# Turning token tiles one by one, and scalar chains moved between quarters, in a hybrid block kernel

## The chip, the cores and the metric

The kernel runs on one core of a Trainium2 chip. The metric is the device time of one execution in microseconds (us); smaller is better. Engines are named as the profile names them: PE (matmul), DVE (VectorE), ACT (ScalarE), POOL (GpSimd), SP (SyncE, which only issues DMAs here). PEld is PE loading its stationary operand.

## What is computed

One layer of a hybrid backbone on 512 latent tokens and 256 context tokens of width 2048, all float32. The part that the change touches is the start:

```
mod_x = silu(c) @ w_ada + b_ada          # (1, 6144): shift, scale, gate
mod_c = silu(c_ctx) @ w_ada + b_ada
h_x = rmsnorm(x, g_pre) * (1 + sc_x) + sh_x       # 512 tokens
h_c = rmsnorm(ctx, g_pre) * (1 + sc_c) + sh_c     # 256 tokens
parts_x = split(h_x @ w_in)                       # u, xa, ba, ca, za, zb, f, zc, gates
u_c = h_c @ w_in[:, u]
a = exp((lam_re + i lam_im) * exp(log_dt))        # 2 x 64 x 64 poles; q = (a - 1) / lam
```

Behind it come a gated convolution, a bidirectional diagonal state-space scan with a GLU, a 2-D Fourier mix, three projections, gates, one output projection, an RMS norm and the residual. They are not touched.

## The kernel before

Products are made three times over, high times high, low times high and high times low, from operands split into a rounded part (`hi`, made by ACT) and the rest (`lo`, made by DVE).

**The opening.** The modulation needs 4 quarters of 512 channels. Quarter q takes eight units of `w_ada`, each 256 rows x 1024 columns (1 MB, two DMAs of 512 KB) in a ring of four buffers, `ring`; SP issues unit n once unit n-4 is used. `ada(n)` (L578, its matmuls are L586) multiplies one unit. After the eighth, ACT copies the sums to `rows` (`rows_cp`), PE turns them to columns (`cols`, L593), and DVE adds the bias and makes shift and scale (`columns(q)`, L1433 to L1438). `ada(8*(q+1))` waits until `columns(q)` has read the bank.

**Tokens.** x arrives in four tiles of 128 tokens (`xn`, 1 MB each), ctx in two (`cn`). ACT squares each tile with a row sum (L1011), DVE makes mean plus epsilon (L1361), ACT the root (L1013), DVE inverts it with one correction step (L1353 to L1357), and ACT scales the tile (L1016). Before the change this is done for all four tiles of x at a time. `early_turn(k)` then turns channel block k of all four tiles (L602) into a PSUM bank of `ac`, and ACT copies it out to `xT` (L1019), for the first 12 of 16 blocks; the last four are turned in quarter 3 by `turn`.

**A quarter of the first product.** For block n of quarter q DVE does `modulate` (L1451; L1455 for ctx), ACT `high`, DVE `low` (L1464); n = 0 to 3 is x, 4 and 5 is ctx. PE does `x_piece(q, r)` (L633, L634, L637) and `c_piece(q, r)` (L650, L651, L653), both with weight units 2q and 2q+1, which ACT rounds (`hi_first`) and DVE subtracts (`lo_first`, L1468). These are units of 512 KB in `wslot`, the first eight issued by SP among the units of `w_ada`. Between the pieces PE takes the ada units of the next quarter.

**Scalar chains on DVE.** The poles need exp, sine and cosine, made of small linked instructions on 128 x 64 elements. Before: both exponentials (L1345, L1347) and the first half of the sines (L1365 to L1374) run ahead of the one `token_scale` for x, the second half (L1377 to L1382) and the cosines (L1386 to L1390) behind it; `zoh` (L1394 to L1408) stands in quarter 0 before its two ctx blocks, `chunk_powers` (L1411 to L1424) at the end of quarter 0. Their results are first read by PE in `p0_z` (L662), behind quarter 3's x pieces.

The order on every engine is the order of the program text; engines meet at semaphores. After the opening come the phases of 'stream', each product one weight unit after another.

Of the kernel before, what the change touches and what calls it, by code (L numbers as in the profile page):

```python
# [24 lines left out]
ALU = mybir.AluOpType  # L25
# [74 lines left out]
def program(nc, x, c, ctx, c_ctx, w_ada, b_ada, g_pre, g_post, w_in, conv_w, lam_re, lam_im, log_dt,  # L100
# [37 lines left out]
    EARLY = 12  # L138
# [52 lines left out]

    hch = at("hch", [128, KD, TC], abr_at, F32R)
    drow = at("drow", [G, L, H], abr_at)
    junk = at("junk", [128, D], abr_at + KD // 2 * TC * 4)
    last4 = (KD - 4) * T * 4
    ring = [at(f"ring{n}", [128, 2, 2, 512], off)
            for n, off in enumerate((hx_at + last4, hxl_at + last4, tab_at, tab_at + 8192))]
# [23 lines left out]
    r = Region(abr_at + 4 * TC * 4)  # L221
    crow = r("crow", [2 * KD, 128])
    vrow = r("vrow", [V_END, 128])
    lam = r("lam", [128, 2, P])
    ldt = r("ldt", [128, 1])
    zt = [r(f"zt{i}", [128, P]) for i in range(8)]
    ei = r("ei", [128, P], I32)
    assert r.p <= abr_at + KD // 2 * TC * 4

    bah = at("bah", [128, KW, T], abr_at, F32R)  # L230
    fT = at("fT", [128, KW * T], abr_at)
# [129 lines left out]
    def _(sp):  # L361
# [19 lines left out]
            sp.dma_start(xn[:, t, :], x[0, t * 128:(t + 1) * 128, :]).then_inc(x_in[t], 16)  # L381
        for n in range(32):
            ada_unit(n)
            if n % 8 >= 6:
                first_unit(n // 8 * 2 + n % 2)
            if n in (8, 9):
                sp.dma_start(cn[:, n - 8, :], ctx[0, (n - 8) * 128:(n - 7) * 128, :]).then_inc(c_in, 16)
# [183 lines left out]
    def _(pe):  # L571
# [6 lines left out]
        def ada(n):  # L578
            q, r = n // 8, n % 8
            if r == 0 and q:  # L580
                pe.wait_ge(col_rd, q)
            pe.wait_ge(ada_in[n % 4], 32 * (n // 4 + 1))
            for kk in range(2):
                for h in range(2):
                    p = 64 * kk + 32 * h
                    last = mm(ss[p:p + 2, 2, :], cs[:, 2 * r + kk, :], ring[n % 4][:, kk, h, :],  # L586
                              start=(r == 0), stop=(r == 7))
            last.then_inc(ada_used, 1)
# [5 lines left out]
                          sel[:, :, :].rearrange("p h s -> p (h s)"), start=True, stop=True)  # L594
            last.then_inc(col_ps, 1)

        def early_turn(k):
            pe.wait_ge(y_done, TT)
            if k >= 4:
                pe.wait_ge(xp_done, k - 3)  # L600
            for t in range(TT):
                last = tr(ac[:, k % 4, t * 128:(t + 1) * 128], xn[:, t, k * 128:(k + 1) * 128], ident[:, :])  # L602
            last.then_inc(xp_ps, 1)

        def turn(q, n):
            if q == 3 or n == 5:
# [73 lines left out]
            last.then_inc(p0_ps, 1)  # L680

        for n in range(8):
            ada(n)
            if n == 3:
                pe.wait_ge(vec_in, 64)
                tr(ss[:, 1, 0:V_END], vrow[:, :], ident[0:V_END, 0:V_END])
                tr(ss[:, 1, 128:128 + G], drow[:, :, :].rearrange("n l h -> n (l h)"), ident[0:G, 0:G]).then_inc(vec_ps, 1)
            if 3 <= n < 7:
                for k in range(3 * (n - 3), 3 * (n - 2)):
                    early_turn(k)  # L690
        cols(0)
        ada(8)
        ada(9)
        pe.wait_ge(xp_done, EARLY)
        for r in range(4):
            x_piece(0, r, range(4))
            ada(10 + r)
        turn(0, 4)
        ada(14)
        turn(0, 5)  # L700
        for q in range(3):
            if q:
                x_piece(q, 0, range(4))
# [265 lines left out]
    def _(act):  # L969
# [26 lines left out]
        def hi_first(u):  # L996
            if u >= 2:
                act.wait_ge(w_used, u - 1)
            act.wait_ge(w_in_s[u % NSLOT], 16 * (u // NSLOT + 1))
            cp(whi[:, u % 2, :], wslot[:, u % NSLOT, :]).then_inc(w_hi, 1)  # L1000
# [5 lines left out]
            act.wait_ge(w_in_s[s], arrived)  # L1006
            cp(whi[:, (U0[k] + j) % 2, :], wslot[:, s, :]).then_inc(w_hi, 1)

        for t in range(TT):
            act.wait_ge(x_in[t], 16)  # L1010
            st.link(a(junk[:, :], toks[t], ACT.Square, accum_out=small[:, 32 + t:33 + t]))  # L1011
        act.wait_ge(var_done, 1)
        a(small[:, 46:50], small[:, 40:44], ACT.Sqrt).then_inc(rt_done, 1)  # L1013
        act.wait_ge(rs_done, 1)
        for t in range(TT):
            cp(toks[t], toks[t], small[:, 52 + t:53 + t]).then_inc(y_done, 1)  # L1016
        for k in range(EARLY):
            act.wait_ge(xp_ps, k + 1)
            cp(xT[:, k, :], ac[:, k % 4, :]).then_inc(xp_done, 1)  # L1019
            if k == 8:  # L1020
                hi_first(0)
        hi_first(1)
        rows_cp(0)
        for n in range(4):
            high(0, n)
        act.wait_ge(c_in, 32)
        for t in range(TT, TT + CT):
            st.link(a(junk[:, :], toks[t], ACT.Square, accum_out=small[:, 32 + t:33 + t]))
        act.wait_ge(var_done, 2)
        a(small[:, 50:52], small[:, 44:46], ACT.Sqrt).then_inc(rt_done, 1)  # L1030
        act.wait_ge(rs_done, 2)
        for t in range(TT, TT + CT):
            cp(toks[t], toks[t], small[:, 52 + t:53 + t]).then_inc(y_done, 1)
        high(0, 4)
# [258 lines left out]
        act.wait_ge(w_in_s[unit(8, 3, 7)[1]], unit(8, 3, 7)[2])  # L1293
        cp(whx[:, :], wslot[:, unit(8, 3, 7)[1], :]).then_inc(w_hi, 1)
        a(small[:, 63:64], ident[:, 0:1], ACT.Sqrt)
        act.wait_ge(var_done, 3)
        for t in range(TT):
            act.wait_ge(ac_done, 9 + t + 1)
            act.wait_ge(sq_done, 12 + t)
# [6 lines left out]
    def _(dve):  # L1306
# [35 lines left out]
        dve.wait_ge(ssm_in, 48)  # L1342
        a0, a1, a2, a3, a4, a5, a6, a7 = [z[:, :] for z in zt]
        lre, lim = lam[:, 0, :], lam[:, 1, :]
        exp(a7[:, 0:1], ldt[:, :], a1[:, 0:1], a2[:, 0:1], a3[:, 0:1], a4[:, 0:1], ei[:, 0:1])  # L1345
        link(ts_(a0, lre, a7[:, 0:1], None, ALU.mult))
        exp(a6, a0, a1, a2, a3, a4, ei[:, :])  # L1347

        def rsqrt(at, n, rt):

            dve.wait_ge(rt_done, rt)
# [7 lines left out]
        def token_scale(at, n, turn):  # L1359
# [2 lines left out]
                .then_inc(var_done, 1)  # L1362
            dve.wait_ge(var_done, turn)
            rsqrt(at, n, turn).then_inc(rs_done, 1)
        link(ts_(a0, lim, a7[:, 0:1], None, ALU.mult))  # L1365
        nearest(a1, a0, 1.0 / math.pi)
        link(stt(a2, a1, -3.140625, a0, ALU.mult, ALU.add))
        link(stt(a2, a1, -9.67502593994140625e-4, a2, ALU.mult, ALU.add))
        link(stt(a2, a1, -1.509957990978376432e-7, a2, ALU.mult, ALU.add))
        nearest(a3, a1, 0.5)  # L1370
        link(stt(a3, a3, -2.0, a1, ALU.mult, ALU.add))
        link(tt(a3, a3, a3, ALU.mult))
        link(ts_(a3, a3, -2.0, 1.0, ALU.mult, ALU.add))
        link(tt(a1, a2, a2, ALU.mult))  # L1374
        fact = [1.0 / math.factorial(n) for n in range(16)]
        token_scale(0, TT, 1)
        link(ts_(a4, a1, fact[13], -fact[11], ALU.mult, ALU.add))  # L1377
        for cc in (fact[9], -fact[7], fact[5], -fact[3], 1.0):
            link(tt(a4, a4, a1, ALU.mult))
            link(ts_(a4, a4, cc, None, ALU.add))  # L1380
        link(tt(a4, a4, a2, ALU.mult))
        link(tt(a4, a4, a3, ALU.mult))  # L1382
        dve.wait_ge(vec_ps, 1)
        cpy(dtab[:, :], ss[:, 1, 128:128 + G])
        link(cpy(vecs[:, :], ss[:, 1, 0:V_END]))
        link(ts_(a5, a1, -fact[14], fact[12], ALU.mult, ALU.add))  # L1386
        for cc in (-fact[10], fact[8], -fact[6], fact[4], -fact[2], 1.0):
            link(tt(a5, a5, a1, ALU.mult))
            link(ts_(a5, a5, cc, None, ALU.add))
        link(tt(a5, a5, a3, ALU.mult))  # L1390
        z = lambda n: ZN[:, n, 0, :]

        def zoh():
# [75 lines left out]
                .then_inc(w_lo, 1)  # L1469

        for q in range(4):
            if q == 0:
                lo_first(0)
            columns(q)
            modulate(q, 0)
            low(q, 0)
            modulate(q, 1)
            low(q, 1)
            if q:
                lo_first(2 * q)  # L1480
            modulate(q, 2)
            low(q, 2)
            modulate(q, 3)
            low(q, 3)
            lo_first(2 * q + 1)
            if q == 0:
                token_scale(TT, CT, 2)
                zoh()
            for n in range(4, 6):
                modulate(q, n)  # L1490
                low(q, n)
            if q == 0:
# [408 lines left out]
        u, s, _ = unit(8, 3, 7)  # L1901
        dve.wait_ge(w_hi, u + 1)
        tt(wlo[:, s, :], wslot[:, s, :], whx[:, :].bitcast(F32), ALU.subtract).then_inc(w_lo, 1)
        dve.wait_ge(var_done, 3)
        dve.wait_ge(xr_in, 64)
        for t in range(TT):
            dve.wait_ge(sq_done, 12 + t + 1)
            tt(Og[:, t, 1536:2048], ss[:, t, :], GG[:, 1536:2048], ALU.mult).then_inc(o_free, 1)
            s40, s46, s52, s58 = (small[:, c0 + t:c0 + t + 1] for c0 in (40, 46, 52, 58))
            link(ts_(s40, ssq[:, 4 * t + 3:4 * t + 4], 1.0 / D, s58, ALU.mult, ALU.add))  # L1910
            dve.wait_ge(rt_done, 3 + t)
            link(v.reciprocal(s52, s46))
# [51 lines left out]
```

## Time and profile before

| | us |
|---|---|
| median of three executions | 2057.66 (2055.9 to 2057.74) |
| profiled execution, device time | 2056.32 |
| its span, first to last instruction | 2054.5 |
| PE busy | 2008.0 (98%) |
| DVE busy | 1085.9 (53%) |
| ACT busy | 594.9 (29%) |
| moved by DMA | 270.72 MB, mean 132 GB/s |

A row of the profile's timeline gives the start and duration in us, the engine, line and operation, written tile <- read tiles, and in brackets how long the engine had been idle and what ended that. A number x8 is a count of instructions merged into the row. Durations of matmuls overlap a little.

### The profile page before, as it was taken

The numbers are of one execution on the slowest core, as the hardware profiler recorded it, in microseconds if no ns is written. First come the engines' busy times: TensorE is split into PE (matmuls) and PEld (weight loads), VectorE is DVE, ScalarE is ACT, GpSimd is POOL, SyncE is SP. The second block draws the span as 40 slices with busy tenths as digits, with TensorE's granted clock in tenths as the row PEclk, the third lists the DMA queues.
The fourth block names the chain that finished last, engine by engine and source line by source line (L and its number), as shares of the span: only waits on it lengthen the run. The fifth ranks groups of instructions, "written<-read, shape, count | busy, mean of one in ns | idle before, by whom it ended". The sixth has DMA issues, their size and how long they took to land.

```text
span 2054.5 us, 26821 instructions
## 1 busy us (share of the span) xinstructions
PE 2008.0 (98%) x10086; PEld 1639.5 (80%) x10086; DVE 1085.9 (53%) x1640; ACT 594.9 (29%) x845; POOL 27.0 (1%) x16
## 2 busy tenths in 40 slices
PE   4999999999999999999999999999999999999998
PEld 1568888888888888888888888888788888888886
DVE  4545799999998645554334344432433333333325
ACT  5325243334333322222222222222322222222222
POOL 0003100000000000000000000000000000000000
PEclk9999999999999999999999999999999999999999
DMA  9963544434344544443334444443233333334423
GB/s 360 365 199 115 167 108 109 104 103 112 98 110 111 179 133 127 128 136 107 102 92 145 127 128 139 129 133 112 62 93 100 95 95 99 93 101 153 173 99 128
DMA packets 384079, 270.72 MB, mean 132 GB/s; under 512 B 24820, under 2 KB 349916, under 8 KB 382164
## 3 DMA queue, kind: packets, MB, share of 16 engines
q1 hardware_dynamic: 373728, 265.61, 41.9%
q10 hardware_dynamic: 10292, 4.33, 1.5%
q8 instruction: 36, 0.59, 0.1%
q14 instruction: 23, 0.19, 0.0%
HBM read 251.81 MB, written 18.09 MB: 131 GB/s over the span
## 4 chain that ended last, share of the span: by engine, by line
PE 93%; DVE 3%; ACT 2%; DMA 1%; issue 1%; SPq 0%; ACTq 0%; DVEq 0%
PE ac L753 25%; PE ac L757 25%; PE ac L754 24%; PE ac L937 1%; PE ac L938 1%; PE ac L936 1%; PE ss L815 1%; PE ss L586 1%; PE ss L938 1%; PE ss L937 1%; PE ss L936 1%; PE ac L633 1%; PE ac L634 1%; PE ac L637 1%; DMA wslot<-w_in 1%
## 5 line engine op out<-in xcount | busy, mean ns | idle before, releaser
L1556 DVE TENSOR_TENSOR wlo<-wslot,whi 128x1024 fp32r<-128x1024 f32 x309 | 378.4, 1224 | 643.4 <-ACT whi L972 639.2
L972 ACT ACTIVATE whi<-wslot 128x1024 fp32r<-128x1024 f32 x327 | 346.9, 1061 | 1244.7 <-PE ac L757 1043.7
L753 PE MATMUL ac<-hxh,whi 128*128 128x512 f32 x1664 | 651.9, 392 | 0.0
L754 PE MATMUL ac<-hxl,whi 128*128 128x512 f32 x1664 | 647.8, 389 | 0.0
L757 PE MATMUL ac<-hxh,wlo 128*128 128x512 f32 x1664 | 411.1, 389 | 0.9 <-DVE wlo L1556 0.9
L753 PEld LDWEIGHTS ac<-hxh,whi 128*128 128x128 f32 x1664 | 312.4, 188 | 67.5 <-issue 2.9
L757 PEld LDWEIGHTS ac<-hxh,wlo 128*128 128x128 f32 x1664 | 312.2, 188 | 66.1 <-DVE wlo L1556 1.3
L754 PEld LDWEIGHTS ac<-hxl,whi 128*128 128x128 f32 x1664 | 312.4, 188 | 63.8
L753 PE MATMUL ac<-bah,whi 128*128 128x512 f32 x384 | 149.4, 389 | 0.0
L754 PE MATMUL ac<-bal,whi 128*128 128x512 f32 x384 | 149.4, 389 | 0.0
L757 PE MATMUL ac<-bah,wlo 128*128 128x512 f32 x384 | 94.8, 389 | 0.0
L753 PEld LDWEIGHTS ac<-bah,whi 128*128 128x128 f32 x384 | 72.1, 188 | 15.0
L754 PEld LDWEIGHTS ac<-bal,whi 128*128 128x128 f32 x384 | 72.1, 188 | 15.0
L757 PEld LDWEIGHTS ac<-bah,wlo 128*128 128x128 f32 x384 | 72.1, 188 | 15.0
L753 PE MATMUL ac<-b2nd,whi 128*128 128x512 f32 x192 | 74.8, 390 | 0.0
L754 PE MATMUL ac<-b2nd,whi 128*128 128x512 f32 x192 | 74.7, 389 | 0.0
L1775 DVE TENSOR_TENSOR gtm<-ac,gsig 128x512 f32<-128x512 f32 x32 | 22.1, 691 | 85.7 <-PE ac L757 85.7
L586 PE MATMUL ss<-ring,cs 128*2 128x512 f32 x256 | 38.1, 676 | 24.1 <-DMA ring<-w_ada 20.8
L1731 DVE SCALAR_TENSOR_TENSOR gacc<-gwt,cs,gacc 128x256 f32<-128x256 f32 x120 | 57.8, 481 | 3.4
L936 PE MATMUL ac<-whi,mhi 128*128 128x512 f32 x128 | 50.2, 392 | 0.0
L938 PE MATMUL ac<-whi,mlo 128*128 128x512 f32 x128 | 49.8, 389 | 0.0
L937 PE MATMUL ac<-wlo,mhi 128*128 128x512 f32 x128 | 49.8, 389 | 0.0
(359 smaller groups left out, 2075.1 us busy)
## 6 DMA issues: line engine op xcount, KB each, us to landing
wslot<-w_in SPq DMA_DIRECT2D x224, 512.0 KB, 3.8
ring<-w_ada SPq DMA_DIRECT2D x64, 512.0 KB, 8.3
gwt<-w_ada SPq DMA_DIRECT2D x128, 128.0 KB, 2.8
wslot<-w_out SPq DMA_DIRECT2D x32, 512.0 KB, 3.6
wslot<-proj_a SPq DMA_DIRECT2D x16, 512.0 KB, 4.1
wslot<-proj_b SPq DMA_DIRECT2D x16, 512.0 KB, 4.1
wslot<-proj_c SPq DMA_DIRECT2D x16, 512.0 KB, 3.9
xn<-x SPq DMA_DIRECT2D x4, 1024.0 KB, 9.7
```

Source lines behind the costliest of these rows:

```text
L586: last = mm(ss[p:p + 2, 2, :], cs[:, 2 * r + kk, :], ring[n % 4][:, kk, h, :], start=(r == 0), stop=(r == 7))
L633: mm(ac[:, m, :], w, hxh[:, k, :], start=(k == 0), stop=False)
L753: mm(ac[:, bank, :], w, xh, start=(v == 0 and q == 0), stop=False)
L754: mm(ac[:, bank, :], w, xl, start=False, stop=False)
L757: last = mm(ac[:, bank, :], wlo[:, s, q * 128:(q + 1) * 128], rhs(v * UNIT + q)[0], start=False, stop=(v == nu - 1 and q == UNIT - 1))
L936: mm(acc[:, t, :], mh, wh, start=(kk == 0), stop=False)
L937: mm(acc[:, t, :], mh, wl, start=False, stop=False)
L938: last = mm(acc[:, t, :], ml, wh, start=False, stop=(kk == KD - 1))
L972: cp = lambda o, i, scale=1.0: nc.scalar.activation(o, i, ACT.Copy, scale=scale)
L1556: tt(wlo[:, s, :], wslot[:, s, :], whi[:, (U0[k] + j) % 2, :].bitcast(F32), ALU.subtract)\
L1731: stt(gacc[:, :], gwt[:, r % 4, :], cs[:, r, 0:1], gacc[:, :], ALU.mult, ALU.add)\
L1775: tt(o if br == 0 else gtm2[:, :], ac[:, (2 * j + 1) % 4, :], gsig[:, :], ALU.mult)\
```

## The change

Four things change. ACT, DVE and PE treat each tile of x by itself: square, root, scale, then twelve transposes of that tile into three banks, `early_turn(t)`, and three copies out. Six banks rotate, four of `ac` and two of `ss`. On PE these stand before ada(0), before ada(1), after ada(2) and after ada(4), and ada(9) moves behind the first x piece (each of the next ones one place later). On SP weight units 0 and 1 both go behind unit 7 of `w_ada`. On ACT and DVE the splits of weight units 0 and 1 move: `hi_first(0)` behind `rows_cp(0)` and ahead of the first `high`, `lo_first(0)` behind the first `modulate`. On DVE the token scales come first, then the exponentials; sines stand at the end of quarter 0, cosines and `zoh` at the end of quarter 1, `chunk_powers` at the end of quarter 2. Two scratch areas move so that they stay free that long.

```diff
-    junk = at("junk", [128, D], abr_at + KD // 2 * TC * 4)
+    junk = at("junk", [128, D], VT_at + KD // 2 * TC * 4)
...
             ada_unit(n)
-            if n % 8 >= 6:
+            if n == 7:
+                first_unit(0)
+                first_unit(1)
+            if n > 8 and n % 8 >= 6:
                 first_unit(n // 8 * 2 + n % 2)
...
-        def early_turn(k):
-            pe.wait_ge(y_done, TT)
-            if k >= 4:
-                pe.wait_ge(xp_done, k - 3)
-            for t in range(TT):
-                last = tr(ac[:, k % 4, t * 128:(t + 1) * 128], xn[:, t, k * 128:(k + 1) * 128], ident[:, :])
-            last.then_inc(xp_ps, 1)
+        PARTS = EARLY // 4
+
+        def early_bank(n):
+            return (ac[:, n % 6, :] if n % 6 < 4 else ss[:, 3 * (n % 6 - 4), :])
+
+        def early_turn(t):
+            pe.wait_ge(y_done, t + 1)
+            for g in range(PARTS):
+                n = t * PARTS + g
+                if n >= 6:
+                    pe.wait_ge(xp_done, n - 5)
+                for k in range(4):
+                    c0 = (4 * g + k) * 128
+                    last = tr(early_bank(n)[:, k * 128:(k + 1) * 128], xn[:, t, c0:c0 + 128], ident[:, :])
+                last.then_inc(xp_ps, 1)
...
         for n in range(8):
+            if n in (0, 1):
+                early_turn(n)
             ada(n)
+            if n in (2, 4):
+                early_turn(n // 2 + 1)
...
-            if 3 <= n < 7:
-                for k in range(3 * (n - 3), 3 * (n - 2)):
-                    early_turn(k)
         cols(0)
         ada(8)
-        ada(9)
-        pe.wait_ge(xp_done, EARLY)
+        pe.wait_ge(xp_done, TT * PARTS)
         for r in range(4):
             x_piece(0, r, range(4))
-            ada(10 + r)
+            ada(9 + r)
         turn(0, 4)
+        ada(13)
+        turn(0, 5)
         ada(14)
-        turn(0, 5)
...
+        token_square(0)
+        token_root(0)
+        token_square(1)
+        token_norm(0)
+        token_root(1)
+        token_square(2)
+        token_norm(1)
+        token_root(2)
+        token_square(3)
+        token_norm(2)
+        token_root(3)
+        early_out(0)
+        token_norm(3)
+        for t in range(1, TT):
+            early_out(t)
+        rows_cp(0)
+        hi_first(0)
+        high(0, 0)
+        high(0, 1)
         hi_first(1)
-        rows_cp(0)
-        for n in range(4):
-            high(0, n)
+        high(0, 2)
+        high(0, 3)
...
+        for t in range(TT):
+            token_scale(t, 1, t + 1)
+        exp(a7[:, 0:1], ldt[:, :], a1[:, 0:1], a2[:, 0:1], a3[:, 0:1], a4[:, 0:1], ei[:, 0:1])
+        link(ts_(a0, lre, a7[:, 0:1], None, ALU.mult))
+        exp(a6, a0, a1, a2, a3, a4, ei[:, :])
...
         for q in range(4):
+            columns(q)
+            modulate(q, 0)
             if q == 0:
                 lo_first(0)
-            columns(q)
-            modulate(q, 0)
             low(q, 0)
...
             if q == 0:
-                token_scale(TT, CT, 2)
-                zoh()
+                token_scale(TT, CT, TT + 1)
             for n in range(4, 6):
                 modulate(q, n)
                 low(q, n)
             if q == 0:
+                sines()
+            if q == 1:
+                cosines()
+                zoh()
+            if q == 2:
                 chunk_powers()
```

## Rows read from the trace of the kernel before

**Rows 1.** The page: busy time of each engine, its share of the span, and instructions.

```profile
PE 2008.0 (98%) x10086; PEld 1639.5 (80%) x10086; DVE 1085.9 (53%) x1640; ACT 594.9 (29%) x845; POOL 27.0 (1%) x16
```

**Rows 2.** Stretches: length, busy (count), clock share, DMA share, GB/s.

```profile
48.00:50.00 2.00, 0.48 (x4) 0.11 (x8) 1.31 (x3) 0.63 (x1) 0.00 (x0) 0.50 0.96 395
...
7.00:76.50 69.50, 49.41 (x276) 24.50 (x276) 35.52 (x144) 38.27 (x43) 0.00 (x0) 0.95 1.04 389
...
80.00:100.00 20.00, 20.00 (x125) 12.08 (x122) 8.93 (x15) 5.05 (x7) 0.00 (x0) 1.00 0.94 337
```

**Rows 3.** Timeline of PE at unit 24 and at the last quarter's wait.

```profile
106.74 0.61 PE L586 MATMUL ss<-ring,cs 128*2 128x512 f32 x4
...
144.22 0.50 PE L637 MATMUL ac<-hxh,wlo 128*128 128x512 f32 x1 [2.12 <-DVE wlo L1468]
```

**Rows 4.** Timeline of DVE at columns(2) and columns(3).

```profile
105.32 0.24 DVE L1433 TENSOR_TENSOR vmod<-ss,vecs 128x8 f32<-128x8 f32 x2 [3.75 <-PE ss L593]
...
132.79 0.24 DVE L1433 TENSOR_TENSOR vmod<-ss,vecs 128x8 f32<-128x8 f32 x2 [3.75 <-PE ss L593]
```

**Rows 5.** Timeline of ACT, the squares, the table load, roots and scales.

```profile
7.72 1.91 ACT L1011 ACTIVATE junk<-xn 128x2048 f32<-128x2048 f32 x1 [1.39 <-DMA xn<-x]
...
21.02 1.28 ACT L1013 ACT_TABLE_LOAD   x1 [2.97 <-DVE small L1361]
...
23.63 7.68 ACT L972 ACTIVATE xn<-xn,small 128x2048 f32<-128x2048 f32 x4 [1.11 <-DVE small L1357]
...
53.29 1.90 ACT L1028 ACTIVATE junk<-cn 128x2048 f32<-128x2048 f32 x1
...
57.61 0.20 ACT L1030 ACTIVATE small<-small 128x2 f32<-128x2 f32 x1 [0.30 <-DVE small L1361]
```

**Rows 6.** Timeline of PE, transposes, and ada(9), ada(10), ada(11) with x pieces between.

```profile
31.36 2.82 PE L602 MATMUL ac<-ident,xn 128*128 128x128 f32 x12 [0.94 <-ACT xn L972]
...
49.52 1.89 PE L586 MATMUL ss<-ring,cs 128*2 128x512 f32 x8 [1.96 <-DMA ring<-w_ada]
...
55.58 1.04 PE L586 MATMUL ss<-ring,cs 128*2 128x512 f32 x8
...
59.49 1.04 PE L586 MATMUL ss<-ring,cs 128*2 128x512 f32 x8
```

**Rows 7.** Second DMA of units 7, 15, 19: last figures are issue start and landing time.

```profile
L367 SPq DMA_DIRECT2D ring<-w_ada x1: 472/472/472, 30.3 to 30.3; - x1
DMA to landing us min/median/max: 9.8/9.8/9.8
...
L367 SPq DMA_DIRECT2D ring<-w_ada x1: 472/472/472, 61.0 to 61.0; - x1
DMA to landing us min/median/max: 8.6/8.6/8.6
...
L367 SPq DMA_DIRECT2D ring<-w_ada x1: 472/472/472, 72.2 to 72.2; - x1
DMA to landing us min/median/max: 9.5/9.5/9.5
```

**Rows 8.** Timeline of PE at units 15 and 16.

```profile
70.70 1.04 PE L586 MATMUL ss<-ring,cs 128*2 128x512 f32 x8
...
79.29 0.61 PE L586 MATMUL ss<-ring,cs 128*2 128x512 f32 x4 [2.95 <-DVE vmod L1433]
```

**Rows 9.** Stretches of the scalar chains: sines (two), cosines, zoh, chunk_powers.

```profile
17.78:20.77 2.99, 1.85 (x8) 0.14 (x8) 2.58 (x12) 0.27 (x2) 0.00 (x0) 1.00 1.05 386
23.51:26.69 3.18, 2.35 (x16) 0.11 (x8) 2.74 (x14) 3.06 (x2) 0.00 (x0) 1.00 1.05 386
30.93:34.34 3.41, 2.98 (x16) 2.53 (x20) 2.94 (x14) 1.69 (x4) 0.00 (x0) 1.00 1.05 386
58.79:62.97 4.18, 4.18 (x23) 2.51 (x22) 3.67 (x16) 3.90 (x2) 0.00 (x0) 1.00 1.05 386
73.67:79.01 5.34, 2.67 (x23) 2.46 (x22) 4.69 (x23) 0.00 (x0) 0.00 (x0) 1.00 1.05 387
```

More of the change, by code:

```diff
@@ L223, in program @@
     vrow = r("vrow", [V_END, 128])
+    assert r.p <= abr_at + KD // 2 * TC * 4
+    r = Region(abr_at + 12 * TC * 4)
     lam = r("lam", [128, 2, P])
@@ L227, in program @@
     ei = r("ei", [128, P], I32)
-    assert r.p <= abr_at + KD // 2 * TC * 4
+    assert r.p <= abr_at + KD * TC * 4
     bah = at("bah", [128, KW, T], abr_at, F32R)
@@ L1007, in hi, with token_square, token_root, token_norm @@
             cp(whi[:, (U0[k] + j) % 2, :], wslot[:, s, :]).then_inc(w_hi, 1)
-        for t in range(TT):
+        def token_square(t):
             act.wait_ge(x_in[t], 16)
             st.link(a(junk[:, :], toks[t], ACT.Square, accum_out=small[:, 32 + t:33 + t]))
[L1012 to L1015, printed above, removed]
-            cp(toks[t], toks[t], small[:, 52 + t:53 + t]).then_inc(y_done, 1)
[L1017 to L1021, printed above, removed]
+        def token_root(t):
+            act.wait_ge(var_done, t + 1)
+            a(small[:, 46 + t:47 + t], small[:, 40 + t:41 + t], ACT.Sqrt).then_inc(rt_done, 1)
+        def token_norm(t):
+            act.wait_ge(rs_done, t + 1)
+            cp(toks[t], toks[t], small[:, 52 + t:53 + t]).then_inc(y_done, 1)
+        def early_out(t):
+            for g in range(EARLY // 4):
+                n = t * (EARLY // 4) + g
+                act.wait_ge(xp_ps, n + 1)
+                bank = ac[:, n % 6, :] if n % 6 < 4 else ss[:, 3 * (n % 6 - 4), :]
+                cp(xT[:, 4 * g:4 * g + 4, t * 128:(t + 1) * 128], bank.rearrange("p (k c) -> p k c", k=4))\
+                    .then_inc(xp_done, 1)
+        token_square(0)
[17 more added lines that the diff above has]
+        high(0, 1)
         hi_first(1)
-        rows_cp(0)
-        for n in range(4):
-            high(0, n)
+        high(0, 2)
+        high(0, 3)
         act.wait_ge(c_in, 32)
@@ L1028, in _ @@
             st.link(a(junk[:, :], toks[t], ACT.Square, accum_out=small[:, 32 + t:33 + t]))
-        act.wait_ge(var_done, 2)
+        act.wait_ge(var_done, TT + 1)
         a(small[:, 50:52], small[:, 44:46], ACT.Sqrt).then_inc(rt_done, 1)
-        act.wait_ge(rs_done, 2)
+        act.wait_ge(rs_done, TT + 1)
         for t in range(TT, TT + CT):
@@ L1295, in _ @@
         a(small[:, 63:64], ident[:, 0:1], ACT.Sqrt)
-        act.wait_ge(var_done, 3)
+        act.wait_ge(var_done, TT + 2)
         for t in range(TT):
@@ L1344, in _ @@
         lre, lim = lam[:, 0, :], lam[:, 1, :]
-        exp(a7[:, 0:1], ldt[:, :], a1[:, 0:1], a2[:, 0:1], a3[:, 0:1], a4[:, 0:1], ei[:, 0:1])
-        link(ts_(a0, lre, a7[:, 0:1], None, ALU.mult))
-        exp(a6, a0, a1, a2, a3, a4, ei[:, :])
         def rsqrt(at, n, rt):
@@ L1364, in token_scale @@
             rsqrt(at, n, turn).then_inc(rs_done, 1)
[L1365 to L1382, printed above, removed]
+        for t in range(TT):
[3 more added lines that the diff above has]
+        exp(a6, a0, a1, a2, a3, a4, ei[:, :])
         dve.wait_ge(vec_ps, 1)
@@ L1385, in _, with sines, cosines @@
         link(cpy(vecs[:, :], ss[:, 1, 0:V_END]))
[L1386 to L1390, printed above, removed]
+        def sines():
+            link(ts_(a0, lim, a7[:, 0:1], None, ALU.mult))
+            nearest(a1, a0, 1.0 / math.pi)
+            link(stt(a2, a1, -3.140625, a0, ALU.mult, ALU.add))
+            link(stt(a2, a1, -9.67502593994140625e-4, a2, ALU.mult, ALU.add))
+            link(stt(a2, a1, -1.509957990978376432e-7, a2, ALU.mult, ALU.add))
+            nearest(a3, a1, 0.5)
+            link(stt(a3, a3, -2.0, a1, ALU.mult, ALU.add))
+            link(tt(a3, a3, a3, ALU.mult))
+            link(ts_(a3, a3, -2.0, 1.0, ALU.mult, ALU.add))
+            link(tt(a1, a2, a2, ALU.mult))
+            fact = [1.0 / math.factorial(n) for n in range(16)]
+            link(ts_(a4, a1, fact[13], -fact[11], ALU.mult, ALU.add))
+            for cc in (fact[9], -fact[7], fact[5], -fact[3], 1.0):
+                link(tt(a4, a4, a1, ALU.mult))
+                link(ts_(a4, a4, cc, None, ALU.add))
+            link(tt(a4, a4, a2, ALU.mult))
+            link(tt(a4, a4, a3, ALU.mult))
+        def cosines():
+            fact = [1.0 / math.factorial(n) for n in range(16)]
+            link(ts_(a5, a1, -fact[14], fact[12], ALU.mult, ALU.add))
+            for cc in (-fact[10], fact[8], -fact[6], fact[4], -fact[2], 1.0):
+                link(tt(a5, a5, a1, ALU.mult))
+                link(ts_(a5, a5, cc, None, ALU.add))
+            link(tt(a5, a5, a3, ALU.mult))
         z = lambda n: ZN[:, n, 0, :]
@@ L1903, in _ @@
         tt(wlo[:, s, :], wslot[:, s, :], whx[:, :].bitcast(F32), ALU.subtract).then_inc(w_lo, 1)
-        dve.wait_ge(var_done, 3)
+        dve.wait_ge(var_done, TT + 2)
         dve.wait_ge(xr_in, 64)
@@ L1910, in _ @@
             link(ts_(s40, ssq[:, 4 * t + 3:4 * t + 4], 1.0 / D, s58, ALU.mult, ALU.add))
-            dve.wait_ge(rt_done, 3 + t)
+            dve.wait_ge(rt_done, TT + 2 + t)
             link(v.reciprocal(s52, s46))
```

## The prediction

> **What bounds the kernel now.** I read the page's totals first: PE is busy for 98% of the span [rows 1], so the whole kernel can gain only where PE stands still, which is 46.5 us in all. Next I read stretches of the opening, where the change lies. From 7 to 76.5 us the DMA engines are full (share 1.04, 389 GB/s) while PE works 49.4 of 69.5 us; from 80 us on PE works without a gap and DMA falls below full [rows 2]. Later, at 144, PE waits again, for DVE. The opening therefore has three limits one after the other: the first DMA queue until some 77 us, then PE, then at the start of the last quarter the pair DVE and ACT.
>
> The third limit is read from PE's row at 144.22: it stood 2.12 us for the low part of weight unit 7 (DVE L1468) [rows 3]. That wait ends a chain which starts at the column step of the last quarter at 132.79 and goes through modulate, rounding on ACT and subtraction on DVE four times [rows 4]. Whatever moves 132.79 moves the rest of the kernel.
>
> **The change part by part, front end.** Before, ACT squares four token tiles as they land (first at 7.72), loads a table at 21.02, scales all four in 7.68 us from 23.63, and only then PE turns them at 31.36 [rows 5, 6]. After the change the rhythm of ACT, with durations from those rows, is: square 0 to 9.7; DVE; table load 1.28 and root to 11.5; square 1 to 13.5; scale 0 (7.68 / 4 = 1.92) to 15.4; then root, square, scale in turn; scale 2 ends at 23.7, copies out of tile 0 (three, 1.6) at 25.4, scale 3 at 27.4, copies of tile 1 at 29.0. PE turns tile 0 from 15.4 to 18.2 (2.82 for twelve [rows 6]), before unit 0 of w_ada is there at all, tile 1 behind ada(0), tile 2 behind ada(2), tile 3 behind ada(4), done by about 35.5. Nothing is saved in number: 48 transposes and 12 copies of 512 columns in both. What is gained is that ada(1) to ada(6) are eaten as they land, and the rest of the turning lies in waits for the DMA queue. DVE pays five small instructions and two waits per tile in place of per four, some 1.3 us each, in ACT's shadow; the two exponentials that now stand behind them (about 10 us) end near 35, and the next DVE work, columns(0), comes after 41, so they cost nothing.
>
> Weight units 0 and 1 now go behind unit 7 instead of one ahead of it. Unit 7 landed at 30.3 + 9.8 = 40.1 [rows 7]; it is 512 KB, 1.35 us, earlier: 38.7. Weight units land at 40.1 and 41.4, later units as before. So ada(7) ends at 39.7, rows and cols(0) at 41.5, columns(0) at 42.0. ACT rounds weight unit 0 at 40.4 to 41.5, ahead of the first high, so nothing is queued badly behind that wait. low(0,0) is done at 44.4 (lo_first(0) now sits ahead of it, 1.2 us), and ada(8), which lands at 44.1, is eaten until 46.0, at the low clock after PE's gap. The first x piece starts at 46.0 instead of 51.4, behind ada(9) at 49.52 + 1.89 [rows 6]: some 5.3 us sooner, partly because ada(9), for which PE waited 1.96 us at 49.52, now stands behind it.
>
> **Why these 5.3 us don't last.** The queue of w_ada was full and in order until 77 us, and carries the same bytes in the same order. Unit 15 landed at 61.0 + 8.6 = 69.6 and unit 19 at 72.2 + 9.5 = 81.7 [rows 7]. Walking PE on with its own durations (x piece and ada 3.91, from 55.58 to 59.49 [rows 6], of it ada 0.97 with the overlap): x pieces 0 to 3 with ada(9) to ada(12) end at 63.6 (the first piece at the low clock, 4.3, and 0.4 us of waiting for unit 10), the two ctx turns and ada(13), ada(14) at 67.0. Then PE waits 2.6 us for unit 15 and ends it at 70.6, where before it ended at 71.7 [rows 6, 8]. The 5.3 us have become 1.1. What is still to be had is the gap at 79.29, where PE stood 2.95 us for DVE, which had chunk_powers (5.34 us) ahead of columns(1) [rows 8, 9]. Sines take its place there: 2.99 + 3.18 = 6.17 us [rows 9], 0.8 more. But they start sooner: the ctx turns come 4.7 us sooner, so DVE is free at 69.0, through with sines at 75.1, and ada(16) can start at 75.4, just as PE comes to it. That is 3.9 us sooner than 79.29. Unit 19, at 81.7, then sets the end: ada(19) ends at 82.65 instead of at 86.3. So 3.65 us are gained on entering the second quarter, and no more than this, since the queue sets it.
>
> **The back end, where it is given back.** cosines (3.41) and zoh (4.18), 7.59 us together [rows 9], move from the first quarter, where they lay beside waits, to between low(1,5) and columns(2). DVE's idle time ahead of columns(2) is 3.75 us [rows 4], so columns(2) comes 3.84 us after its natural place, at 105.32 + 3.84 - 3.65 = 105.5. PE needs it for ada(24): that ran at 106.74 [rows 3], 1.14 us after the 105.60 at which the columns were read, and now comes at 105.8. PE's lead shrinks from 3.65 to 0.95. Then chunk_powers, 5.34 us, stands ahead of columns(3), again in an idle stretch of 3.75 us [rows 4]: 1.59 us too long. This delay falls right on the third limit. Columns(3) comes at 132.79 + 1.59 - 0.95 = 133.4. Sum: 3.84 - 1.14 + 1.59 - 3.65 = **+0.64 us**. I take nothing for what follows: the chain of that quarter has the same instructions, and ZN is ready long before p0_z.
>
> Unknown prices. The early copies out write 128-column pieces at a stride instead of one run; from no extra to double (0.5 us each), they stay in ACT's slack ahead of 39.7. PE's clock in the new order isn't in the trace: nothing to 2.6 us, below. The lead could be 0.5 us more if the queue's rate varies; a gain beyond the queue is excluded, because bytes and order are the same.
>
> Two rules of the Trainium skill speak against parts of this. ScalarE: Activation LUTs, section "Table sets: the hidden batching unit", says to batch activations by set and not by function, since a change of set costs a load. The rows show Square at 53.29 and 55.31 and Sqrt at 57.61 with no load between, after the one at 21.02 [rows 5], so alternating costs none here; with a load at each of six changes, 6 x 1.28 = 7.7 us, tile 3 would be turned by 43 and the first x piece would start some 3 us later, which the wait for unit 15 takes up. DMA: Bandwidth & Descriptors, section "Specifications", gives about 358 GB/s from HBM for a core; an estimate from that page would land unit 19 six us later. The trace disagrees with 389 GB/s, and the measurement decides.
>
> **Rivals.**
> Low clock, slower: in the trace PE fell to half clock (0.50 at 48 to 50 us) after broken work around 44 to 49 and was back near 55 [rows 2, 6]. The new order has new gaps, at 41.5 to 44.1 and at 67.0 to 69.6. One spell after the second gap, as long as the old one, costs about 2.5 us: 2060.0. If instead the clock stays low through the x pieces, each piece with its ada takes 7.1 instead of 3.9 us, by the ratio of the two adas at either level (1.89 to 1.04 [rows 6]); four cost 12.8, less 2.6 of waiting: 10.2 later than the forecast, 2067.7. It decides from the point at which two of the four pieces run low. Against it: the same pieces brought the clock back within one piece before, and 2.95 us of idling at 76 to 79 didn't lower it. 9% for over +4.1, 10% for the one spell.
> The gaps are as wide as the moved chains: then 3.65 us stay, 2053.3, just inside 0.2%. Against it are the two idle times of 3.75 us [rows 4]. 6%.
> The queue doesn't bind: the 5.3 us, and the 2.12 us at 144, are kept: 2051.6 to 2049.5. Against it is a full DMA share until 77. 5%.
>
> **How the numbers follow.** 0.2% is 4.1 us, about what a measurement of this kernel can tell from no change. The profiled execution took 2056.32 us (span 2054.5, 1.8 around it), 1.3 below the median 2057.66; the mean of the four executions shown is 2056.9. With +0.64 on it: **2057.5 us**, essentially no change, 70%. Same is 70 + 10 + 6 less a little for scatter at the edges: 82%. Faster 7%, slower 11%. The range goes from the rival that keeps its gain, with a little scatter, to the one clock spell with 1 us of scatter: 2053.5 to 2061.5.
>
> **What would show it.** Right: first x piece near 46; PE waits 2 to 3 us for ring ahead of ada(15); no idle of PE for vmod near 75; ada(24) waits about 2.7 us for DVE's column step (vmod); DVE has no idle time ahead of columns(2) and columns(3); the wait for the low part of weight unit 7 ends at 144.9 or so. Wrong: PE still idle for DVE in the first quarter, half clock over more than one piece between 46 and 70, or the last quarter's columns well before 132.

## The result

The changed kernel takes 2061.85 us (median of 22 executions, 2059.03 to 2064.23), the kernel before 2058.51 us (22, 2055.90 to 2062.93). The ratio is 1.0014, with a 95% interval from 1.0008 to 1.0020: slower by some 3 us. The forecast was 2057.5 us and no change, with a range that ended at 2061.5. The time lies above the range. Two executions of the kernel before in the later comparisons, at 4160 and 6281 us, are left out of every figure below.

The traces are of single executions. That of the kernel before took 2056.32 us, 2.2 us under its median, and that of the kernel after 2059.82 us, 2.0 us under its own, so the two can be set beside each other, and both are on the fast side.

Read beside the first rows is the page of the kernel after: its span, then busy time of each engine. PE is busy 2.5 us more [rows 1] with the same 10086 instructions, and stands still 1.0 us more.

```profile
span 2058.0 us, 26840 instructions
...
PE 2010.5 (98%) x10086; PEld 1643.3 (80%) x10086; DVE 1088.7 (53%) x1658; ACT 594.9 (29%) x848; POOL 27.0 (1%) x16
```

The same instructions, busy for longer in sum, point to some of them having run slower. The timeline of ACT in the kernel after shows the new opening; it answers rows 5.

```profile
7.21 1.91 ACT L1025 ACTIVATE junk<-xn 128x2048 f32<-128x2048 f32 x1 [0.73 <-DMA xn<-x]
...
9.55 1.28 ACT L1029 ACT_TABLE_LOAD   x1 [0.34 <-DVE small L1396]
...
12.97 2.00 ACT L986 ACTIVATE xn<-xn,small 128x2048 f32<-128x2048 f32 x1
...
24.45 2.01 ACT L986 ACTIVATE xn<-xn,small 128x2048 f32<-128x2048 f32 x1
```

One table load, then square, root and scale in turn, without another load. The timeline of PE in the kernel after, which answers rows 6, 8 and 3:

```profile
44.07 1.89 PE L591 MATMUL ss<-ring,cs 128*2 128x512 f32 x8 [1.02 <-DMA ring<-w_ada]
46.02 0.77 PE L646 MATMUL ac<-hxh,whi 128*128 128x512 f32 x1
...
69.39 1.04 PE L591 MATMUL ss<-ring,cs 128*2 128x512 f32 x8 [2.72 <-DMA ring<-w_ada]
...
105.62 1.51 PE L591 MATMUL ss<-ring,cs 128*2 128x512 f32 x8 [2.57 <-DVE vmod L1477]
...
117.14 1.04 PE L591 MATMUL ss<-ring,cs 128*2 128x512 f32 x8
...
146.06 0.50 PE L650 MATMUL ac<-hxh,wlo 128*128 128x512 f32 x1 [2.13 <-DVE wlo L1512]
...
157.84 0.93 PE L675 MATMUL ss<-ident,ZN 128*128 128x128 f32 x7
```

Read down the idle times in brackets. The first x piece starts at 46.0, 5.3 us sooner than before, where its first matmul was at 51.33. PE waits 2.72 us for unit 15. ada(16), at 75.07 and without a bracket, no longer waits. ada(24) waits 2.57 us for DVE's columns. p0_z, the first work behind the opening, starts at 157.84; in the kernel before it started at 154.38. These 3.46 us are the whole difference of the spans, 2058.0 - 2054.5: from p0_z to the end both kernels take the same time, 1900.1 and 1900.2 us.

The timeline of DVE in the kernel after, at columns(2) and columns(3), answers rows 4: there is no idle time ahead of either, so no bracket.

```profile
105.33 0.24 DVE L1477 TENSOR_TENSOR vmod<-ss,vecs 128x8 f32<-128x8 f32 x2
...
134.39 0.42 DVE L1468 COPY ZN<-ZN 128x448 f32<-128x448 f32 x1
134.74 0.22 DVE L1477 TENSOR_TENSOR vmod<-ss,vecs 128x8 f32<-128x8 f32 x2
```

columns(2) is where it was before, 105.33 for 105.32. columns(3) is 1.95 us later.

What is new is in the stretches. The columns are those of rows 2; the third figure from the end is the granted clock of PE. First the kernel after, then the kernel before over the same work (from ada(24) to ada(28), and from the last quarter's wait to p0_z).

```profile
106.00:109.40 3.40, 3.40 (x19) 2.34 (x12) 2.01 (x4) 2.21 (x3) 0.00 (x0) 0.51 0.28 74
...
147.00:150.40 3.40, 3.40 (x12) 2.78 (x11) 1.47 (x3) 0.63 (x1) 0.00 (x0) 0.50 0.00 0
...
105.62:117.14 11.52, 11.52 (x68) 6.74 (x68) 7.11 (x11) 4.42 (x6) 0.00 (x0) 0.85 0.71 238
146.06:157.84 11.78, 11.78 (x49) 9.62 (x50) 3.38 (x6) 2.84 (x5) 0.00 (x0) 0.86 0.01 1
```

```profile
106.74:116.72 9.98, 9.98 (x69) 5.68 (x68) 6.41 (x9) 4.13 (x6) 0.00 (x0) 1.00 0.82 270
...
144.22:154.38 10.16, 10.16 (x48) 8.35 (x49) 3.37 (x6) 2.84 (x5) 0.00 (x0) 1.00 0.01 2
```

Soon behind each of the two waits, of 2.57 and 2.13 us, PE ran at half clock (0.50, the 1.2 GHz level) for a while. It began 0.4 us after the first wait had ended and 1.0 us after the second. The same work took 11.52 us for 9.98 and 11.78 for 10.16: 1.54 and 1.62 us more. The kernel before had a wait of 2.12 us at the second place too [rows 3], and in its profiled execution no half clock behind it.

The 3.46 us of p0_z are then: ada(24) 1.12 sooner, 1.54 of low clock, 1.42 lost between ada(28) and the end of the last quarter's wait (1.84 late there, 0.42 at ada(28)), and 1.62 of low clock: -1.12 + 1.54 + 1.42 + 1.62 = 3.46. The 1.42 is chunk_powers' excess, forecast at 1.59.

### The profile page after: what moved, and what is told of

Its sections match the earlier page's. It is cut to its first block, busy times and chain, and to the rows that moved or that the text cites. A ratio compares the mean times of both kernels' runs of the same rounds, so it can differ in the third digit from the quotient of the medians.

```text
span 2058.0 us, 26840 instructions
## 1 busy us (share of the span) xinstructions
PE 2010.5 (98%) x10086; PEld 1643.3 (80%) x10086; DVE 1088.7 (53%) x1658; ACT 594.9 (29%) x848; POOL 27.0 (1%) x16
## 4 chain that ended last, share of the span: by engine, by line
PE 91%; DMA 4%; DVE 3%; ACT 1%; issue 1%; SPq 1%; DVEq 0%; ACTq 0%
PE ac L767 25%; PE ac L771 25%; PE ac L768 24%; DMA ring<-w_ada 3%; PE ac L951 1%; PE ac L952 1%; PE ac L950 1%; PE ss L829 1%; PE ss L952 1%; PE ss L951 1%; PE ss L950 1%; PE ss L591 1%; DMA wslot<-w_in 1%; PE ss L822 1%; PE ac L646 1%
## 5 line engine op out<-in xcount | busy, mean ns | idle before, releaser
L951 PE MATMUL ss<-wlo,mhi 128*128 128x512 f32 x128 | 49.8, 389 | 0.0
```

Source lines behind the costliest of these rows:

```text
L951: mm(acc[:, t, :], mh, wl, start=False, stop=False)
```

## The experiments

The theory after the result (A) has three parts: the front end gives what was forecast; the chains cost what was forecast, because DVE's idle stretches at the ends of the quarters are shorter than the chains are; and the rest is half clock behind PE's waits. Rivals: B, turning tile by tile upsets what follows and the chains are harmless; C, the half clock has another cause than these waits, or costs nothing.

**The front end alone.** The changed kernel, with the chains called where they had been:

```diff
+        sines()
         dve.wait_ge(vec_ps, 1)
         cpy(dtab[:, :], ss[:, 1, 128:128 + G])
         link(cpy(vecs[:, :], ss[:, 1, 0:V_END]))
+        cosines()
...
                 token_scale(TT, CT, TT + 1)
+                zoh()
...
-            if q == 0:
-                sines()
-            if q == 1:
-                cosines()
-                zoh()
-            if q == 2:
-                chunk_powers()
+            if q == 0:
+                chunk_powers()
```

> The changed kernel with the scalar chains called where the kernel before had them: sines and cosines ahead of columns(0), zoh ahead of the ctx blocks of quarter 0, chunk_powers at its end. Nothing is left out. Theory A (the chains in the narrow gaps cost 2.70 and 1.59 us, and the two spells of half clock behind PE's waits at 103 and 144 us cost 1.4 and 1.6): the lead of the front end, 3.65 us on entering quarter 1, is kept to the end, PE doesn't wait ahead of ada(24), no half clock at 106 to 109; 3 to 4 us below before, ratio 0.998 to 0.9985. Theory B (turning tile by tile itself upsets what follows, the chains are harmless): ratio stays at 1.001.

Measured: 2056.0 us (11 executions), ratio 0.9985 (0.9976 to 0.9995), as expected by theory A. The front end is a gain, and PE doesn't wait ahead of ada(24). But the expectation said that the lead is kept to the end, and in the profiled execution it isn't, for its stretches show half clock again, at other places:

```profile
71.60:78.40 6.80, 6.80 (x36) 6.28 (x38) 5.40 (x22) 0.92 (x2) 0.00 (x0) 0.50 1.05 386
...
143.40:146.60 3.20, 3.20 (x10) 2.53 (x10) 0.59 (x2) 0.00 (x0) 0.00 (x0) 0.50 0.00 0
```

The first is behind the wait for unit 15. With it ada(16) starts at 78.00, where in the kernel after it starts at 75.07. The second is behind the last quarter's wait, and p0_z comes at 154.89, 0.5 us later than in the kernel before. B falls, for it has the ratio stay at 1.001 here.

**The chains alone.** The kernel before with the same four blocks at the ends of quarters 0, 1 and 2 and the two scratch areas moved with them. Nothing of the front end.

> The kernel before with the scalar chains alone moved, as in the change. Nothing is left out. Theory A: 0.8 us later in quarter 0 (6.17 for 5.34), 2.7 at ada(24), 1.6 at columns(3), together 5.1, and 1 to 3 us of half clock: 5 to 8 us above before, ratio 1.0025 to 1.004. Theory B: within 1 us of before.

Measured: 2065.6 us (6 executions, 2065.20 to 2067.43), ratio 1.0031 (1.0019 to 1.0043), some 6 us more, within the 5 to 8 that theory A expected. Waits of PE in its timeline:

```profile
79.45 1.13 PE L588 MATMUL ss<-ring,cs 128*2 128x512 f32 x8 [3.79 <-DVE vmod L1439]
...
110.98 1.89 PE L588 MATMUL ss<-ring,cs 128*2 128x512 f32 x8 [2.56 <-DVE vmod L1439]
```

3.79 for 2.95 in quarter 0 is the 0.8 us of sines over chunk_powers; 2.56 is the 2.7 at ada(24), and its 1.89 us for eight matmuls is the low clock. Its profiled execution has three such spells, behind these two waits and behind the last quarter's, of 2.12 us:

```profile
80.20:83.60 3.40, 3.40 (x20) 2.74 (x20) 2.03 (x4) 2.21 (x3) 0.00 (x0) 0.51 0.59 145
110.98:114.40 3.42, 3.42 (x15) 1.71 (x16) 2.00 (x5) 2.21 (x3) 0.00 (x0) 0.50 0.17 16
151.80:155.20 3.40, 3.40 (x12) 2.77 (x11) 0.99 (x2) 0.26 (x1) 0.00 (x0) 0.52 0.00 0
```

The two parts add up: -0.0015 and +0.0031 make +0.0016, and the whole change gives +0.0014. Each of these carries an uncertainty of about 0.001, so an interplay of more than some 3 us between the parts is excluded, and a smaller one isn't.

**PE's waits filled.** PE gets matmul work that nobody reads, in a PSUM bank that is free then, just ahead of the wait. It takes nothing away and costs nothing as long as it ends before the wait does; in this run 0.38 us of the wait ahead of ada(24) are left behind it.

```diff
+            if n == 24:
+                pe.wait_ge(ht_done, 12)
+                for _ in range(20):
+                    tr(ss[:, 3, 0:128], ident[:, :], ident[:, :])
             if r == 0 and q:
                 pe.wait_ge(col_rd, q)
...
+            if q == 3 and r == 2 and ms == (0,):
+                pe.wait_ge(col_rd, 4)
+                for _ in range(16):
+                    tr(ss[:, 2, 0:128], ident[:, :], ident[:, :])
             pe.wait_ge(w_lo, u + 1)
```

> The changed kernel; PE fills two of its waits with transposes that nobody reads: 20 ahead of its wait for columns(2) before ada(24) (2.4 of 2.57 us), 16 ahead of its wait for the low part of weight unit 7 in the last quarter (1.9 of 2.13 us). Theory A: the granted clock stays at full level at 106 to 109 us and 146 to 150 us; ada(28) starts some 1.4 us sooner than at 117.14, and the whole is 2.5 to 3 us below the changed kernel, within 1 us of before. Rival C (half clock comes from something else than these waits, or their cost is hidden by DVE): same time as the changed kernel, ratio 1.0014, and the clock falls as before or its fall costs nothing.

Measured: 2060.56 us (11), ratio 1.0007 (0.9998 to 1.0016). Both spells are gone from the profiled execution and p0_z is at 155.96, but a new one sits behind the wait for unit 15, which was not filled, so that ada(16) starts at 76.79 for 75.07:

```profile
71.30:74.70 3.40, 3.40 (x17) 3.36 (x16) 2.92 (x15) 0.12 (x1) 0.00 (x0) 0.50 1.06 388
```

The expectation of 2.5 to 3 us was met by half, and the profiled execution shows a place for the rest. So the third wait was filled as well, by 20 transposes into a bank of `ss` ahead of the wait for unit 15:

> The changed kernel; PE fills three waits: 20 transposes at unit 15 (2.4 of 2.6 us), 20 ahead of ada(24), 16 in the last quarter. Nobody reads them. Theory A: with no half clock between 60 us and the last product, only the walk of the prediction is left, +0.64 us against the kernel before without half clock: p0_z near 155.0, and 0.5 to 1 us above before_filled. Rival (the front end or the chains cost more than their durations): 2 us or more above before_filled.

Measured: 2058.37 us (11), ratio 0.9999 (0.9990 to 1.0008). Its stretches show full clock throughout the opening:

```profile
62.00:110.00 48.00, 46.85 (x327) 29.46 (x326) 28.92 (x87) 10.35 (x15) 0.00 (x0) 1.00 0.96 351
...
100.00:140.00 40.00, 37.42 (x260) 26.54 (x258) 25.21 (x70) 8.55 (x13) 0.00 (x0) 1.00 0.76 237
140.00:160.00 20.00, 19.62 (x121) 17.15 (x122) 10.54 (x29) 6.66 (x10) 0.20 (x1) 1.00 0.12 32
```

p0_z is at 154.79. Against 154.38 in the profiled execution of the kernel before, which was free of half clock after 60 us, that is +0.4 us, where the walk of the forecast gave +0.64. This is no sharp test, for single executions of one kernel are shifted against each other by as much: ada(24) starts at 105.62 in one trace of the changed kernel and at 106.39 in the other. Three fillers took the ratio of the changed kernel from 1.0014 (1.0009 in the second measurement, below) to 0.9999, 2 to 3 us, without taking any work away, and the spells behind these waits are gone from the trace. C falls.

**The kernel before filled.** 23 transposes ahead of ada(16)'s wait, 16 in the last quarter.

> The kernel before; PE fills two of its waits with transposes that nobody reads: 23 ahead of its wait for columns(1) at ada(16) (2.7 of 2.95 us), 16 ahead of the wait for the low part of weight unit 7 (1.9 of 2.12 us). If half clock behind these waits, now here and now there, is what spreads the executions of the kernel before over 2055 to 2063 us, this one lies at 2055.5 to 2058 with less spread, ratio 0.999. If not, the same median and spread as before.

Measured: 2056.53 us (11 executions, 2055.88 to 2057.98), ratio 0.9990 (0.9981 to 0.9999), beside 2058.05 (2055.71 to 2063.02) of the unfilled one on the same chip. So the kernel before has such spells too in many executions, and few of them in its fastest. The mean granted clock that is recorded with every execution says the same: among the 31 of the kernel before in this comparison it was 0.997 or 0.998 where they took 2055.7 to 2057.9 us, and 0.993 where they took 2062.6 to 2063.0. Likewise the 22 of the changed kernel go from 0.996 at 2059.8 us to 0.991 at 2064.2. The mean says how much low clock there was, not where. The four executions from which the forecast started, with a mean of 2056.9, were on the lucky side.

after_filled3 lies 1.8 us above before_filled, over the 0.5 to 1 that was expected, and close to the rival's 2 or more. In the profiled executions p0_z is no later for it, 154.79 against 155.16, so the difference isn't seen in the opening. Its executions fall in two groups, four at 2056.3 to 2056.8, level with before_filled, and seven at 2058.3 to 2059.2. The profiled execution is of the lower group. The next two kernels show a place for the 2 us between the groups.

**chunk_powers alone moved.** It is called in quarter 2 ahead of the ctx blocks, in place of behind them; otherwise as after_filled3.

> after_filled3 with chunk_powers alone moved from the end of quarter 2 to ahead of its ctx blocks, where DVE idled 5.72 us. Theory A: columns(3) is ready when PE's cols(3) is, 1.6 us sooner, and all that follows with it: 1.6 us below after_filled3. If the last quarter is set by PE and not by DVE's chain: 0.

Measured: 2056.65 us (11), ratio 0.9991 (0.9982 to 1.0000), 1.7 us below after_filled3, where 1.6 were expected; columns(3) at 132.10 for 133.28, and p0_z at 153.66 for 154.79. This execution had started ada(24) 0.4 us later; counted from there, columns(3) is 1.6 us sooner and p0_z 1.5. Its executions fall in two groups as well, of five and six, and the profiled one, of the slower group, has half clock at a place outside the opening, behind a wait of 1.94 us ahead of the Fourier products:

```profile
1455.20:1458.60 3.40, 3.40 (x19) 3.40 (x18) 1.05 (x6) 0.72 (x3) 0.00 (x0) 0.52 0.11 32
```

after_filled3's profiled execution has the same wait and full clock behind it.

**The chains in the wide stretches.** DVE idles longest ahead of the ctx blocks, while PE works on x pieces 0 and 1.

```diff
             if q == 0:
                 token_scale(TT, CT, TT + 1)
+                sines()
+            if q == 1:
+                zoh()
+            if q == 2:
+                chunk_powers()
             for n in range(4, 6):
                 modulate(q, n)
                 low(q, n)
             if q == 0:
-                sines()
-            if q == 1:
                 cosines()
-                zoh()
-            if q == 2:
-                chunk_powers()
```

> The changed kernel with the chains in DVE's wide idle stretches, that ahead of the ctx blocks: sines (6.17 us) in quarter 0 ahead of block 4 (6.66 idle), cosines (3.41) at the end of quarter 0 (4.6 idle), zoh (4.18) in quarter 1 ahead of block 4 (4.96 idle), chunk_powers (5.34) in quarter 2 ahead of block 4 (5.72 idle). Theory A: all of it is hidden, the lead of 3.65 us is kept, columns(3) starts near 129.1: 3.5 to 4.5 us below before, ratio 0.998. Theory B: ratio 1.000 or above. If half clock spells stay without the waits: some 1.5 us less gain.

Measured: 2056.53 us (11 executions, 2052.49 to 2058.84), ratio 0.9987 (0.9977 to 0.9997). Expected were 3.5 to 4.5 us, measured 2.0 to 2.7. The timeline of DVE shows that the chains are hidden, with idle time left behind each: sines, cosines (ahead of columns(1)), `zoh` and chunk_powers, in this order:

```profile
64.35 1.00 DVE L1499 TENSOR_SCALAR htmp<-ss,vmod 128x256 f32<-128x256 f32 x2 [0.64 <-PE ss L633]
...
75.46 0.24 DVE L1477 TENSOR_TENSOR vmod<-ss,vecs 128x8 f32<-128x8 f32 x2 [3.14 <-PE ss L598]
...
92.78 0.99 DVE L1499 TENSOR_SCALAR htmp<-ss,vmod 128x256 f32<-128x256 f32 x2 [1.72 <-PE ss L633]
...
120.16 1.00 DVE L1499 TENSOR_SCALAR htmp<-ss,vmod 128x256 f32<-128x256 f32 x2 [0.25 <-PE ss L633]
```

It times like the front end alone (2056.0 us beside it), and p0_z is at 154.96 for 154.89 there, so the chains cost nothing that these runs can tell. The missing part is half clock again, behind the waits at unit 15 and in the last quarter, as its stretches show:

```profile
71.70:78.50 6.80, 6.80 (x35) 6.23 (x37) 2.66 (x9) 0.97 (x2) 0.00 (x0) 0.50 1.05 387
143.40:146.80 3.40, 3.40 (x11) 2.72 (x11) 0.74 (x2) 0.00 (x0) 0.00 (x0) 0.50 0.00 0
```

These two waits filled:

> wide_gaps with the waits at unit 15 and in the last quarter filled (20 and 16 transposes). Theory A: the whole lead of the front end stays, 3.65 us below before_filled, p0_z at 150.7; executions at 2052 to 2054, ratio to before 0.9965 to 0.998, with a smaller spread than wide_gaps (2052.5 to 2058.8). If the queue of w_ada doesn't set the lead, more than 4.5 us below before_filled.

Measured: 2053.55 us (9 executions, 2052.04 to 2055.64), ratio 0.9974 (0.9965 to 0.9984); p0_z at 151.20. The lead stays: 3.0 us below before_filled, where 3.65 were expected. But its profiled execution took 2053.9 - 151.2 = 1902.7 us from p0_z to the end, where after_filled3 took 1899.7. One stretch of wide_filled2 below full clock lies there:

```profile
1440.00:1460.00 20.00, 18.07 (x97) 15.88 (x95) 5.88 (x13) 5.59 (x11) 0.00 (x0) 0.91 0.28 79
```

and in its timeline the wait in it, ahead of the Fourier products:

```profile
1452.96 0.68 PE L901 MATMUL ss<-dftw,fP 128*128 128x129 f32 x4 [1.93 <-ACT fT L993]
```

It is the place that chunk_early_filled3 showed. From this wait to the end it took 600.9 us for 599.2 in after_filled3, so the spell makes 1.7 of the 3.0 us; the rest lies ahead of it, at full clock, and isn't explained. All versions have this wait. It was filled last:

```diff
+        pe.wait_ge(yb_cp, NB)
+        for _ in range(15):
+            tr(ss[:, 0, 0:128], ident[:, :], ident[:, :])
         for a in range(4):
             freed(pe, 5, 1, a)
```

> wide_filled2 with one more wait of PE filled: 15 transposes (1.8 of 1.93 us) ahead of the Fourier products at 1453 us, where wide_filled2 showed half clock in its profiled execution and the other filled kernels' times fall in two groups 2 us apart. If that spell is what is left of the scatter: all executions within 1.5 us, 2052 to 2053.5, median about 1 us below wide_filled2's 2053.55. If not: the same scatter as wide_filled2 (2052.0 to 2055.6).

Measured: 2052.79 us, ratio 0.9973 (0.9961 to 0.9984), and all 7 executions between 2052.39 and 2053.23, where the kernel before spread over 7 us. The expectation was a spread within 1.5 us and a median 1 us lower; it is 0.8 lower. This version beats both kernels, by about 6 us and 8 us. Its stretches:

```profile
72.00:140.00 68.00, 66.41 (x443) 45.20 (x443) 37.99 (x91) 17.17 (x24) 0.00 (x0) 1.00 0.92 308
140.00:150.00 10.00, 9.62 (x48) 7.81 (x47) 4.02 (x7) 2.84 (x5) 0.00 (x0) 1.00 0.01 2
```

**The changed kernel once more**, beside wide_filled3:

> The changed kernel without any edit, on the same chip as wide_filled3. Theory A: ratio to before 1.001 to 1.002 as first measured, some 8 us above wide_filled3, and its profiled execution again shows one or two spells of half clock behind PE's waits at unit 15, ada(24) or the last quarter, not always the same ones.

Measured: 2060.57 us (11), ratio 1.0009 (1.0000 to 1.0018), 7.8 us above wide_filled3. The profiled execution shows the same two spells, behind 2.57 us of waiting at ada(24) and 2.12 us in the last quarter:

```profile
106.70:110.10 3.40, 3.40 (x18) 2.14 (x11) 2.01 (x4) 2.21 (x3) 0.00 (x0) 0.50 0.23 39
147.70:151.10 3.40, 3.40 (x12) 2.71 (x11) 1.30 (x3) 0.63 (x1) 0.00 (x0) 0.50 0.00 0
```

That they sit at the same two places twice is a hint that the order of waits draws them, not chance alone. The wait of 2.65 us for unit 15 had no half clock behind it, again as in the first trace; the expectation that the places vary was not borne out here.

## Why the prediction was wrong

Its walk, step by step, against the profiled execution of the kernel after:

| step | forecast | measured |
|---|---|---|
| first x piece | 46.0 | 46.02 |
| wait for unit 15 | 2.6 | 2.72 |
| unit 19 lands | 81.7 | 70.9 + 10.6 = 81.5 |
| ada(16) | 75.4 | 75.07 |
| columns(2) | 105.5 | 105.33 |
| wait ahead of ada(24) | 2.7 | 2.57 |
| ada(24) | 105.8 | 105.62 |
| columns(3) | 133.4 | 134.74 |
| last quarter's wait ends | 144.9 | 146.06 |
| p0_z | 154.38 + 0.64 = 155.0 | 157.84 |

Up to ada(24) every step is within 0.4 us. The landing of unit 19 is from its row:

```profile
L369 SPq DMA_DIRECT2D ring<-w_ada x1: 470/470/470, 70.9 to 70.9; - x1
...
DMA to landing us min/median/max: 10.6/10.6/10.6
```

**The queue of w_ada as the limit** was right: the 5.3 us of the first x piece shrink to the landings. Of the lead, 3.65 us were forecast on entering the second quarter. ada(19) started at 81.58 behind 0.28 us of waiting for the queue, and so ended at 82.6 for 86.3: 3.7 us. wide_filled2 and wide_filled3 keep 3.2 and 3.5 us of it to the end of the opening, with p0_z at 151.2 and 150.8 for 154.4.

**The chains in the gaps** were right in mechanism and size: 0.8 and 2.6 in the kernel with the chains alone, 1.5 to 1.7 for chunk_powers. The forecast's sum without the clock, +0.64, is +0.4 in the filled kernel's profiled execution, give or take the shift between single executions. Its measured median lies 1.8 us above before_filled. Half clock ahead of the Fourier products, as chunk_early_filled3 and wide_filled2 show it, is the size of the gap between its two groups, but no trace of its slower group was taken, and why before_filled has no such groups stays open.

**The step that failed** is the term of the sum that was put at nothing: "I take nothing for what follows", with the clock only as a rival, and at the wrong waits. In the trace it is 1.54 + 1.62 = 3.2 us of half clock. The forecast itself placed a new wait of 2.7 us at ada(24), and knew the one of 2.12 us in the last quarter, but asked about the clock only behind the waits at 41.5 and 67.0. A reason given was that PE idled 2.95 us at 76 to 79 in the trace of before without a fall. One execution that shows none is thin: executions of the same kernel lay 7 us apart, and this scatter was to be had only as 1.8 us from three of them. The price per spell, "about 2.5 us", was given without its working; measured are 1.4 to 1.6, and 2.7 for the long one behind unit 15 (in front_alone ada(15) to ada(16) took 8.4 us for 5.7). One spell was given 10%; two were not considered.

**The starting point** was low as well: the mean of four executions, 2056.9, against a median of 2058.5 in 22. +0.64 on that would be 2059.1; the other 2.7 us go to the spells that the changed kernel has in excess of the kernel before, as the two traces show them; for the untraced executions that is argued from their mean clock.

The ends of the range don't follow from what they are said to come from. The lower one, 2053.5, lies above the 2053.3 of the rival that keeps its gain, and the upper one should be 2060.0 and 1 of scatter, 2061.0 in place of 2061.5.

## What to carry to other kernels

Work that is moved into idle time of an engine has to be shorter than the one stretch it lands in, not than the engine's idle time in sum; the same chains cost some 6 us at the ends of the quarters, half clock included, and nothing that could be measured once three of them stood two blocks earlier. A lead that is won ahead of a full DMA queue is worth only what the queue's landings leave of it. And a wait of PE of 2 to 3 us costs more than its length where the clock falls behind it, so ask for each wait that a change makes or keeps what runs behind it; filling such waits with matmuls that nobody reads took 1.5 to 3 us off three versions of this kernel. It took most of the scatter of two of them, and of the changed kernel's less than half.

## What the runs showed of the hardware

PE's granted clock fell to half behind waits of 1.57 to 3.79 us, once as the wait ended (at 110.9 in chains_alone) and otherwise 0.2 to 2.0 us into the work behind it. The same wait did so in one kernel and not in another: 2.72 and 2.65 us at unit 15 in the two traces of the changed kernel without a fall, 1.57 to 2.6 us at the same place in three others with one. The clock came back by itself while PE worked on; the low stretches shown above are of 3.2 to 6.8 us, at a cost of 1.4 to 2.7 us. This is most of what spreads executions of the kernel before over 2055.7 to 2063.0 us: with two of its waits filled they lie within 2.1 us, and in the best version, with three filled, within 0.84 us. TensorE: Matmul & The Clock Gate in the Trainium skill says in its section "HAM oscillation — how this bites in real kernels" that waits for data can throttle PE so that the next work starts cold. The runs here agree that waits do this, with waits of 1.57 to 3.79 us, but for the start: mostly the next work began at full clock and the fall came up to 2.0 us later. What in the order of waits decides whether it falls was not tried and stays open.
